# Expert down products in 32- and 64-token tiles, with another order of the last scatter and the last layer norm, in a one-core encoder layer

## Chip, cores and metric

One core of a Trainium2 chip (trn2) runs the whole program. The metric is the device time of one execution in microseconds (us); it stood at a median of 1172.59 us over 3 runs (1171.43 to 1172.86) before the change. All data are float32.

## What is computed

An encoder layer over two sequences that share all weights: a prompt of 256 tokens and a sample of 512 tokens, width 1024. In front stand a layer norm, an input projection, attention heads beside a two-way state-space scan, an output projection and a layer norm. The part that the change touches is the last one, the mixture of experts and the norm behind it:

```python
def _expert_choice(h, w_router, w_gate, w_up, w_down):
    n_tok, d = h.shape
    cap = CAPACITY_FACTOR * n_tok // N_EXPERTS
    aff = jax.nn.softmax((h @ w_router).astype(jnp.float32), axis=-1)
    gate, idx = lax.top_k(aff.T, cap)
    xe = h[idx]
    hid = jax.nn.silu(jnp.einsum("ecd,edf->ecf", xe, w_gate)) * jnp.einsum("ecd,edf->ecf", xe, w_up)
    ye = jnp.einsum("ecf,efd->ecd", hid, w_down) * gate[..., None].astype(h.dtype)
    return jnp.zeros_like(h).at[idx.reshape(-1)].add(ye.reshape(-1, d))
...
    moe = _expert_choice(x.reshape(b * s, d), w_router, w_e_gate, w_e_up, w_e_down).reshape(b, s, d)
    ple = jax.nn.sigmoid(x @ w_ple_gate + b_ple_gate) * (p @ w_ple)
    return _layer_norm(DN_ALPHA * x + moe + ple, ln2_g, ln2_b)
```

There are 16 experts of 1024 x 1024 weights for gate, up and down. Each expert takes its 32 best prompt tokens and its 64 best sample tokens, 96 rows together.

## The kernel before

The tokens are six tiles of 128: two of the prompt (TP = 2), four of the sample. `x1_rows` and `acc_rows` are arrays in HBM. `acc_rows` holds, for every token, everything that the last norm will read: it starts as the scaled residual plus the gated embedding, and the experts' rows are added to it.

For each expert the engines pass a piece of work on, ordered by semaphores alone, in hand-written loops (one `Fori` on each engine):

- **SP** issues the weight loads: four quarters of gate and up weights (`load_gu`, 2 MB each, into four buffers `gu_w`), two halves of the down weights (`load_dn`, 2 MB each, into two buffers `dn_w`). A load waits until TensorE has finished with what is in its buffer (`s_ug` for a quarter, `s_ud` for a half).
- **POOL** gathers the 96 rows from `x1_rows` (`gather`) and later scatters the expert's output rows with an add (`scatter`, L683).
- **PE** (TensorE) turns the gathered rows (`rows_turn`, L1911), multiplies by gate and up (`gate_up`, L1933), turns the hidden rows (`hid_turn`, L1919) and multiplies by down (`down_half`, L1945).
- **ACT** applies silu (L996) and copies turned rows (L728); **DVE** multiplies silu and up (`hidden`, L1419), copies the turned hidden rows (`hid_out`, L1413) and multiplies the down products by the gates (`ye_out`, L1426).

The 96 rows are three groups of 32. A product has 128 contraction rows, 32 stationary columns (the tokens) and a slice of the weights as moving operand; four such products, one for each quarter of the weight columns, write PSUM partitions 0, 32, 64 and 96 and run side by side in four column tiles of the array. In `down_half`:

```python
for i in range(4):
    k = 4 * d + i
    for g in range(NG3):
        for j in range(CT):
            last = nc.tensor.matmul(ps[32 * j:32 * (j + 1), DN + g, 0:256], src[:, k, 32 * g:32 * (g + 1)],
                                    dn_w[d][:, i, 256 * j:256 * (j + 1)], start=(k == 0), stop=(k == KD - 1))
```

That is 8 x 3 x 4 = 96 products an expert. Partition 32 j + t of a group holds quarter j of token t's output row, so a scatter of one group writes 128 pieces of 256 elements; there are three scatters an expert. The turns (L1911, L1919) use the array whole (128 columns).

The down weights of expert 15 go into the same two buffers `dn_w`, each when `down` of expert 14 has finished with it. `hid_turn` of expert 15 stands between the halves of `down` of expert 14. When all scatters have landed, SP loads the six tiles of `acc_rows` into `fin`, and the last norm runs through them: DVE statistics (`stats_half`, `moments`, `variance`), a square root on ACT (L1011), DVE `inverse` and `shift`, one pass on ACT (L1013), two halves of the gain on DVE (L1467), the bias on POOL (L715, the last tile on DVE, L1498), and the store (L558).

Of the kernel before, what the change touches and what calls it, by code (L numbers as in the profile page):

```python
# [20 lines left out]
ALU = mybir.AluOpType  # L21
# [7 lines left out]
P = 128  # L29
# [36 lines left out]
def hymba_layer(nc, A, consts, out_prompt, out_sample):  # L66
# [8 lines left out]
    NG3 = CAP // 32  # L75
    PADW = TP * P + TS * P + 6
# [6 lines left out]
    with ctx:  # L83
        def sb(name, shape, dt=F32):
            return ctx.enter_context(nc.sbuf_tensor(name, shape, dt))
# [41 lines left out]
        jcol = sb("jcol", [P, 1])  # L127
        idx4 = sb("idx4", [P, NG3, NE], I32)
        idxT = sb("idxT", [CAP, NE], I32)
        idx_now = sb("idx_now", [P, 1 + NG3], I32)  # L130
# [64 lines left out]
        gate4 = att[:, 0, 0:NG3 * NE].rearrange("p (i e) -> p i e", i=NG3)  # L195
# [7 lines left out]
        dn_w = [slot[j].rearrange("p (k c) -> p k c", k=4) for j in (5, 2)]  # L203

# [137 lines left out]
        s_bn = sem("s_bn")  # L342
        s_mv = sem("s_mv")
        s_inv = sem("s_inv")
        s_ln_s = sem("s_ln_s")
        s_ln_z = sem("s_ln_z")
        s_ln_g = sem("s_ln_g")
        s_y2 = sem("s_y2")
        s_y2_last = sem("s_y2_last")
# [85 lines left out]
        def _(sp):  # L435
# [108 lines left out]
            for d in range(2):  # L544
                sp.wait_ge(s_ud, 2 * (NE - 2) + d + 1)
                load_dn(NE - 1, d)

            sp.wait_ge(s_scat, 16 * NG3 * NE)
            for t in range(NT):
                sp.dma_start(fin[:, t, :], acc_rows[t * P:(t + 1) * P, :]).then_inc(s_fin[t], 16)  # L550
            for t in range(NT):
                if t + 1 < NT:
                    sp.wait_ge(s_y2, t + 1)
                else:
                    sp.wait_ge(s_y2_last, 1)
# [10 lines left out]
        def _(pool):  # L566
            ch = Chain(pool, s_pool)
            ch.link(nc.gpsimd.memset(ones[:], 1.0))
            for j in range(CT):
                ch.link(nc.gpsimd.memset(jcol[32 * j:32 * (j + 1), :], float(j)))  # L570
# [110 lines left out]
            def scatter():  # L681
                for i in range(NG3):
                    pool.indirect_dma_start(acc_quarters,  # L683
                                            bass.IndirectOffsetOnAxis(ap=idx_now[:, 1 + i:2 + i], axis=0),
                                            ye[:, i, :], None, compute_op=ALU.add).then_inc(s_scat, 16)
# [4 lines left out]
            def pick_quarters(e):  # L690
                return nc.gpsimd.tensor_copy(idx_now[:, 1:1 + NG3].unsqueeze(2), idx4[:, :, bass.ds(e, 1)])  # L691
# [16 lines left out]
            for e in (NE - 3, NE - 2, NE - 1):  # L708
# [10 lines left out]
        def _(act):  # L719
# [289 lines left out]
            for t in range(NT):  # L1009
                root()  # L1010
                nc.scalar.activation(sd[:, 0, t:t + 1], sd[:, 0, t:t + 1], ACT.Sqrt).then_inc(s_std, 1)  # L1011
                act.wait_ge(s_ln_s, t + 1)
                nc.scalar.activation(fin[:, t, :], fin[:, t, :], ACT.Identity, bias=mv[:, t, 1:2],  # L1013
                                     scale=sd[:, 1, t:t + 1]).then_inc(s_ln_z, 1)
# [3 lines left out]
        def _(dve):  # L1018
# [366 lines left out]
            for (a, n), c0, cap in ((SEQS[0], 0, CAPP), (SEQS[1], CAPP, CAPS)):  # L1385
                lo, hi = a * P, (a + n) * P
                for k in range(cap // 8):
# [6 lines left out]
                    if rounds % 4 == 0:  # L1394
# [8 lines left out]
            nc.vector.tensor_scalar(idx4[:].rearrange("p i e -> p (i e)"), ps[:, 5, NE:(1 + NG3) * NE], float(CT), jcol[:, 0:1],  # L1403
                                    ALU.mult, ALU.add).then_inc(s_idx, 1)
            nc.vector.tensor_copy(att[:, 0, 0:NG3 * NE], ps[:, 5, (1 + NG3) * NE:(1 + 2 * NG3) * NE]).then_inc(s_idx, 1)
# [15 lines left out]
            def ye_out(e, at_e, first=False):  # L1421
                dve.wait_ge(s_ud, 2 * (e + 1))
                if not first:
                    dve.wait_ge(s_scat, 16 * NG3 * e)
                for i in range(NG3):
                    last = nc.vector.tensor_scalar(ye[:, i, :], ps[:, DN + i, 0:256], gate4[:, i, at_e], None,  # L1426
                                                   ALU.mult)
                last.then_inc(s_ye, 1)
# [10 lines left out]
            ye_out(NE - 1, slice(NE - 1, NE))  # L1439

            def stats_half(t, half):
                dve.wait_ge(s_fin[t], 16)
                nc.vector.bn_stats(stats[:, t % 2, 6 * half:6 * half + 6],
                                   fin[:, t, half * 512:(half + 1) * 512]).then_inc(s_bn, 1)

            def moments(t):
                dve.wait_ge(s_bn, 2 * t + 2)
                nc.vector.bn_aggr(mv[:, t, :], stats[:, t % 2, :]).then_inc(s_mv, 1)

            def variance(t):  # L1450
                dve.wait_ge(s_mv, t + 1)
                nc.vector.tensor_scalar(sd[:, 0, t:t + 1], mv[:, t, 1:2], LN_EPS, None, ALU.add).then_inc(s_var, 1)

            def inverse(t):
                nroot[0] += 1
                dve.wait_ge(s_std, nroot[0])
                nc.vector.reciprocal(sd[:, 1, t:t + 1], sd[:, 0, t:t + 1]).then_inc(s_inv, 1)

            def shift(t):
                dve.wait_ge(s_inv, t + 1)  # L1460
                nc.vector.tensor_scalar(mv[:, t, 1:2], mv[:, t, 0:1], sd[:, 1, t:t + 1], -1.0, ALU.mult,
                                        ALU.mult).then_inc(s_ln_s, 1)

            def gain_half(t, half):
                dve.wait_ge(s_ln_z, t + 1)
                c = slice(half * 512, (half + 1) * 512)
                ins = nc.vector.tensor_tensor(fin[:, t, c], fin[:, t, c], gB[:, c], ALU.mult)  # L1467
                if half:
                    ins.then_inc(s_ln_g, 1)

            dve.wait_ge(s_ln2, 32)
            stats_half(0, 0)
            stats_half(0, 1)
            moments(0)
            variance(0)
            stats_half(1, 0)
            inverse(0)
            stats_half(1, 1)
            shift(0)
            moments(1)  # L1480
            variance(1)
            for t in range(NT):
                if t + 2 < NT:
                    stats_half(t + 2, 0)
                if t + 1 < NT:
                    inverse(t + 1)
                if t + 2 < NT:
                    stats_half(t + 2, 1)
                if t + 1 < NT:
                    shift(t + 1)  # L1490
                gain_half(t, 0)
                if t + 2 < NT:
                    moments(t + 2)
                gain_half(t, 1)
                if t + 2 < NT:
                    variance(t + 2)
            dve.wait_ge(s_ln_g, NT)
            nc.vector.tensor_tensor(fin[:, NT - 1, :], fin[:, NT - 1, :], bB[:], ALU.add).then_inc(s_y2_last, 1)  # L1498
# [3 lines left out]
        def _(pe):  # L1502
# [394 lines left out]
            for v, src in enumerate((topf, topv)):  # L1897
                for i in range(NG3):
                    c = (1 + v * NG3 + i) * NE
                    for j in range(CT):  # L1900
                        last = nc.tensor.matmul(ps[32 * j:32 * (j + 1), 5, c:c + NE], src[:, i * 32:(i + 1) * 32],
                                                ident[0:NE, 0:NE], start=True, stop=True)
# [35 lines left out]

            def down_half(e, d, src):
                pe.wait_ge(s_dnw[d], 16 * (e + 1))  # L1940
                for i in range(4):
                    k = 4 * d + i
                    for g in range(NG3):
                        for j in range(CT):
                            last = nc.tensor.matmul(ps[32 * j:32 * (j + 1), DN + g, 0:256],  # L1945
                                                    src[:, k, 32 * g:32 * (g + 1)],
                                                    dn_w[d][:, i, 256 * j:256 * (j + 1)],
                                                    start=(k == 0), stop=(k == KD - 1))
                last.then_inc(s_ud, 1)
# [34 lines left out]
            down(NE - 1, xeT)  # L1984
# [27 lines left out]
```

## Time and profile before

| what | us |
|---|---|
| median of 3 runs | 1172.59 (1171.43 to 1172.86) |
| the profiled execution's own time | 1173.55 |
| its span, first to last instruction | 1171.6 |
| PE busy (share of the span) | 1057.4 (90%) |
| DVE busy | 441.1 (38%) |
| POOL busy | 287.7 (25%) |
| ACT busy | 255.4 (22%) |
| start of expert 0's gate and up products | 591.25 |
| end of the last down product | 1128.32 |

The page is one execution. "Busy" is time with at least one instruction on the engine; PE is the matrix products, PEld the loads of their stationary operand, which overlap them. A product here is recorded twice, so 96 products are 192 records. "x1 (96*128)" shapes read as contraction rows * stationary columns, then the moving operand. The chain of waits is followed back from the last instruction; the timeline lists instructions by their start, neighbours of one line merged.

### The profile page before, as it was taken

How to read it: one execution, taken by the hardware profiler on the slowest of the kernel's cores; microseconds unless marked ns; L12 is line 12 of the kernel's file. 1: busy time of each engine (PE TensorE's matmuls, PEld its weight loads, DVE VectorE, ACT ScalarE, POOL GpSimd, SP SyncE). 2: the span in 40 equal slices, each digit the busy share in tenths (PEclk: the TensorE clock that was granted, in tenths of full speed). 3: DMA queues.
4: the chain of work that ended last, by engine and by line, in shares of the span. 5: the costliest groups of instructions: out<-in, count | busy, mean ns of one | idle time of the engine just before them, and what ended most of it. 6: DMA issues, size and time to landing. Idle time of an engine off the chain costs nothing.

```text
span 1171.6 us, 20620 instructions
## 1 busy us (share of the span) xinstructions
PE 1057.4 (90%) x8753; PEld 600.2 (51%) x8753; DVE 441.1 (38%) x872; ACT 255.4 (22%) x534; POOL 287.7 (25%) x311
## 2 busy tenths in 40 slices
PE   5999778878999899898999999999999999999940
PEld 3568667665565587665633334444443334444420
DVE  5436785447777876675100101111101101111018
ACT  1143334266556611320110000000000000000002
POOL 0006994234554200000100212221012212220134
PEclk9999998979999999999999999999999999999975
DMA  9010200200000531404189999999999999999854
GB/s 339 14 51 22 72 1 1 74 34 1 1 1 1 170 127 54 180 27 180 41 333 400 391 386 391 384 398 401 388 390 399 390 385 387 394 399 404 325 157 176
DMA packets 63116, 254.00 MB, mean 217 GB/s; under 512 B 7383, under 2 KB 15447, under 8 KB 46686
## 3 DMA queue, kind: packets, MB, share of 16 engines
q1 hardware_dynamic: 52542, 234.48, 51.3%
q0 software_dynamic: 10528, 18.88, 6.5%
q8 instruction: 31, 0.51, 0.2%
q14 instruction: 15, 0.12, 0.0%
HBM read 237.62 MB, written 15.73 MB: 216 GB/s over the span
## 4 chain that ended last, share of the span: by engine, by line
PE 67%; DVE 13%; DMA 9%; POOL 6%; issue 2%; ACT 2%; SPq 0%; DVEq 0%; POOLq 0%; ACTq 0%
PE ps L1933 24%; PE ps L1945 11%; DMA ring<-in_w_e_up 7%; PE ps L1574 4%; PE ps L1680 2%; PE ps L1695 2%; PE ps L1568 2%; PE ps L1828 1%; PE ps L1785 1%; PE ps L1787 1%; PE ps L1786 1%; PE ps L1813 1%; PE ps L1814 1%; PE ps L1815 1%; DVE xT L1467 1%
## 5 line engine op out<-in xcount | busy, mean ns | idle before, releaser
L1933 PE MATMUL ps<-ring,mix 128*32 128x512 f32 x1536 | 170.7, 592 | 2.1 <-DMA ring<-in_w_e_up 2.1
L1933 PE MATMUL ps<-late,mix 128*32 128x512 f32 x1536 | 171.1, 593 | 0.0
L1419 DVE TENSOR_TENSOR mix<-mix,ps 128x768 f32<-128x768 f32 x16 | 15.3, 954 | 323.0 <-ACT mix L996 323.0
L996 ACT ACTIVATE mix<-ps 128x768 f32<-128x768 f32 x16 | 13.0, 811 | 480.3 <-PE ps L1933 480.3
L1933 PEld LDWEIGHTS ps<-ring,mix 128*32 128x32 f32 x1536 | 49.6, 110 | 117.9 <-issue 111.9
L1933 PEld LDWEIGHTS ps<-late,mix 128*32 128x32 f32 x1536 | 48.1, 110 | 109.1 <-issue 106.8
L1945 PE MATMUL ps<-late,mix 128*32 128x256 f32 x1536 | 87.9, 385 | 2.8 <-DMA late<-in_w_e_down 2.8
L1945 PE MATMUL ps<-ring,mix 128*32 128x256 f32 x1536 | 85.9, 379 | 0.0
L1426 DVE TENSOR_SCALAR mix<-ps,att 128x256 f32<-128x256 f32 x48 | 20.3, 478 | 161.7 <-PE ps L1945 161.7
L683 POOL DMA_INDIRECT acc_rows<-mix,idx_now x48 | 75.0, 1562 | 20.5 <-POOL idx_now L691 10.7
L1945 PEld LDWEIGHTS ps<-late,mix 128*32 128x32 f32 x1536 | 49.9, 111 | 35.5 <-DVE mix L1413 3.2
L1945 PEld LDWEIGHTS ps<-ring,mix 128*32 128x32 f32 x1536 | 50.5, 110 | 32.3 <-issue 0.2
L688 POOL COPY idx_now<-idxT 96x1 int32 (+1 forms) x14 | 2.5, 182 | 221.1 <-PE ps L1911 221.1
L691 POOL COPY idx_now<-idx 128x3 int32 (+1 forms) x16 | 3.0, 186 | 194.5 <-DVE mix L1426 194.5
L1574 PE MATMUL ps<-ring,xT 128*128 128x512 f32 x96 | 45.2, 626 | 1.2 <-ACT xT L728 1.2
L1657 PE MATMUL ps<-xT 128*128 128x512 f32 (+1 forms) x96 | 45.0, 555 | 1.3 <-issue 1.3
L1548 PE MATMUL ps<-xl,wh 128*128 128x512 f32 (+1 forms) x128 | 44.0, 344 | 0.0
L1813 PE MATMUL ps<-ring_r,xT_r 128*128 128x512 f32 x96 | 40.4, 421 | 1.6 <-DVE cst L1359 1.6
L852 ACT ACTIVATE ring<-ps,att 128x512 f32<-128x512 f32 (+1 forms) x48 | 29.4, 612 | 48.9 <-DVE att L1190 48.8
L1099 DVE SCALAR_TENSOR_TENSOR late<-late,cw 128x770 f32<-128x770 f32 x32 | 39.2, 1227 | 0.9
L1671 PE MATMUL ps<-cst,ring 128*128 128x128 f32 x160 | 28.0, 291 | 11.3 <-DVE gb_in L1198 5.4
L1814 PE MATMUL ps<-late_r,xT_r 128*128 128x512 f32 x96 | 37.5, 391 | 0.0
(295 smaller groups left out, 1793.0 us busy)
## 6 DMA issues: line engine op xcount, KB each, us to landing
late<-in_w_e_gate SPq DMA_DIRECT2D x32, 1024.0 KB, 19.2
late<-in_w_e_up SPq DMA_DIRECT2D x32, 1024.0 KB, 21.3
ring<-in_w_e_gate SPq DMA_DIRECT2D x32, 1024.0 KB, 18.7
ring<-in_w_e_up SPq DMA_DIRECT2D x32, 1024.0 KB, 20.9
late<-in_w_e_down SPq DMA_DIRECT2D x16, 2048.0 KB, 22.3
ring<-in_w_e_down SPq DMA_DIRECT2D x16, 2048.0 KB, 22.2
ring<-in_w_in SPq DMA_DIRECT2D x3, 2048.0 KB, 9.0
late<-in_w_ple_gate SPq DMA_DIRECT2D x2, 2048.0 KB, 14.1
```

The lines of the kernel that those rows point to most:

```text
L683: pool.indirect_dma_start(acc_quarters, bass.IndirectOffsetOnAxis(ap=idx_now[:, 1 + i:2 + i], axis=0), ye[:, i, :], None, compute_op=ALU.a ...
L852: nc.scalar.activation(prob[:, u % 4, 0:L], ps[:, u % 3, 0:L], ACT.Exp, bias=att[:, 0, u:u + 1], scale=HD ** -0.5, accum_out=att[:, 1, u:u ...
L1099: ins = nc.vector.scalar_tensor_tensor(conv[:, m, :], u_pad[:, m, j:j + CW], cw[:, m, j:j + 1], conv[:, m, :], ALU.mult, ALU.add)
L1548: nc.tensor.matmul(o, w_h, xl[:, k, a * P:(a + w) * P], start=False, stop=False)
L1568: last = nc.tensor.matmul(bank[:, 0:272], lhs[k], wkv[:, k, :], start=(k == 0), stop=(k == KD - 1))
L1574: last = nc.tensor.matmul(bank, lhs[k], slotk[0][:, k, :], start=(k == 0), stop=(k == KD - 1))
L1657: nc.tensor.matmul(ps[:, u % 3, 0:n * P], qT[:, h % 4, t * P:(t + 1) * P], kz[:, h // 4, a * P:(a + n) * P], start=True, stop=True).then_i ...
L1671: last = nc.tensor.transpose(ps[:, 3, b * P:(b + 1) * P], prob[:, u % 4, b * P:(b + 1) * P], ident)
L1813: nc.tensor.matmul(o, x_h, wpg_h[h][:, k, :], start=(k == 0), stop=False)
L1814: nc.tensor.matmul(o, x_h, wpg_l[h][:, k, :], start=False, stop=False)
L1933: last = nc.tensor.matmul(ps[32 * j:32 * (j + 1), GU + g, :].rearrange("p (w c) -> p w c", w=2), xeT[:, k, 32 * g:32 * (g + 1)], gu_w[q][: ...
L1945: last = nc.tensor.matmul(ps[32 * j:32 * (j + 1), DN + g, 0:256], src[:, k, 32 * g:32 * (g + 1)], dn_w[d][:, i, 256 * j:256 * (j + 1)], st ...
```

## The change

Four edits. The down products of an expert are made in two groups instead of three: the 32 prompt tokens as before, in four tiles of 32 columns with 256 moving columns, and the 64 sample tokens in two tiles of 64 columns with 512 moving columns. There are two scatters an expert: 128 pieces of 256 elements and 128 pieces of 512. The down weights of expert 15 are loaded into two of the gate and up buffers, once expert 15's own first two quarters are used. Expert 15 makes all prompt products first; its prompt rows are scaled, scattered, loaded and normed ahead of its sample rows. The last norm is two `scalar_tensor_tensor` passes over a tile on DVE; its statistics come from DVE for the first tile of each sequence and from ACT, by two accumulating passes, for the other four; POOL does none of it.

```diff
@@ names @@
-        hid, ye = [r.rearrange("p (i c) -> p i c", i=NG3) for r in rows[2:4]]
-        acc_quarters = acc_rows.rearrange("t (j c) -> (t j) c", j=CT)
+        hid = rows[2].rearrange("p (i c) -> p i c", i=NG3)
+        ye = (rows[3][:, 0:256], rows[3][:, 256:768])
+        acc_parts = (acc_rows.rearrange("t (j c) -> (t j) c", j=4), acc_rows.rearrange("t (j c) -> (t j) c", j=2))
...
+        dn_last = [slot[j].rearrange("p (k c) -> p k c", k=4) for j in (3, 0)]
@@ SP @@
             for d in range(2):
-                sp.wait_ge(s_ud, 2 * (NE - 2) + d + 1)
-                load_dn(NE - 1, d)
-
-            sp.wait_ge(s_scat, 16 * NG3 * NE)
+                sp.wait_ge(s_ug, 4 * (NE - 1) + d + 1)
+                sp.dma_start(dn_last[d], wd[NE - 1, :, 4 * d:4 * d + 4, :]).then_inc(s_dn_last[d], 16)
+
+            for i, tiles in enumerate((range(TP), range(TP, NT))):
+                sp.wait_ge(s_scat, 16 * NSC * (NE - 1))
+                sp.wait_ge(s_scat_last[i], 16)
+                for t in tiles:
+                    sp.dma_start(fin[:, t, :], acc_rows[t * P:(t + 1) * P, :]).then_inc(s_fin[t], 16)
@@ POOL @@
-            pool.wait_ge(s_scat, 16 * NG3 * NE)
-            for t in range(NT - 1):
-                pool.wait_ge(s_ln_g, t + 1)
-                nc.gpsimd.tensor_tensor(fin[:, t, :], fin[:, t, :], bB[:], ALU.add).then_inc(s_y2, 1)
+            pool.wait_ge(s_scat, 16 * NSC * (NE - 1))
+            ch.link(pick_quarters(NE - 1))
+            for i in range(NSC):
+                pool.wait_ge(s_ye, NE + i)
+                pool.indirect_dma_start(acc_parts[i], bass.IndirectOffsetOnAxis(ap=idx_now[:, 1 + i:2 + i], axis=0),
+                                        ye[i], None, compute_op=ALU.add).then_inc(s_scat_last[i], 16)
@@ ACT @@
+            def row_mean(t):
+                act.wait_ge(s_fin[t], 16)
+                ch.link(nc.scalar.activation(junk, fin[:, t, :], ACT.Copy, accum_out=mv[:, t, 0:1]))
+                ch.link(nc.scalar.activation(mv[:, t, 1:2], mv[:, t, 0:1], ACT.Copy, scale=-1.0 / D))
+
+            def row_std(t):
+                ch.link(nc.scalar.activation(junk, fin[:, t, :], ACT.Square, bias=mv[:, t, 1:2],
+                                             accum_out=sd[:, 0, t:t + 1]))
+                nc.scalar.activation(sd[:, 0, t:t + 1], sd[:, 0, t:t + 1], ACT.Sqrt, bias=epsc[:],
+                                     scale=1.0 / D).then_inc(s_std, 1)
+
+            x_std(0)
+            row_mean(1)
+            row_std(1)
+            row_mean(TP + 1)
+            x_std(TP)
+            row_std(TP + 1)
+            for t in range(TP + 2, NT):
+                row_mean(t)
+                row_std(t)
@@ DVE @@
-            ye_out(NE - 1, slice(NE - 1, NE))
...
+            dve.wait_ge(s_scat, 16 * NSC * (NE - 1))
+            for i, w in enumerate((256, 512)):
+                dve.wait_ge(s_ud, 2 * NE - 1 + i)
+                nc.vector.tensor_scalar(ye[i], ps[:, DN + i, 0:w], gate4[:, i, NE - 1:NE], None,
+                                        ALU.mult).then_inc(s_ye, 1)
+
+            def last_norm(t):
+                nroot[0] += 1
                 dve.wait_ge(s_std, nroot[0])
...
+                ch.link(nc.vector.reciprocal(sd[:, 1, t:t + 1], sd[:, 0, t:t + 1]))
+                mean, op = (mv[:, t, 0:1], ALU.subtract) if t in (0, TP) else (mv[:, t, 1:2], ALU.add)
+                ch.link(nc.vector.scalar_tensor_tensor(fin[:, t, :], fin[:, t, :], mean, gB[:], op, ALU.mult))
+                nc.vector.scalar_tensor_tensor(fin[:, t, :], fin[:, t, :], sd[:, 1, t:t + 1], bB[:], ALU.mult,
+                                               ALU.add).then_inc(s_y2, 1)
...
             for t in range(NT):
...
+                if t in (0, TP):
+                    dve.wait_ge(s_fin[t], 16)
+                    ln_stats(t, fin[:, t, :], LN_EPS)
+                last_norm(t)
@@ PE @@
+            def down_step(g, k, src, w):
+                rows = (32, 64)[g]
+                cols = D * rows // P
+                for j in range(P // rows):
+                    last = nc.tensor.matmul(ps[rows * j:rows * (j + 1), DN + g, 0:cols], src[:, k, ROWS[g]],
+                                            w[:, cols * j:cols * (j + 1)], start=(k == 0), stop=(k == KD - 1))
+                return last
+
             def down_half(e, d, src):
                 pe.wait_ge(s_dnw[d], 16 * (e + 1))
                 for i in range(4):
...
+                    down_step(0, 4 * d + i, src, dn_w[d][:, i, :])
+                    last = down_step(1, 4 * d + i, src, dn_w[d][:, i, :])
                 last.then_inc(s_ud, 1)
...
-            down(NE - 1, xeT)
+            pe.wait_ge(s_hT, NE)
+            pe.wait_ge(s_ye, NE - 1)
+            for g in range(NSC):
+                for k in range(KD):
+                    if k % 4 == 0:
+                        pe.wait_ge(s_dn_last[k // 4], 16)
+                    last = down_step(g, k, xeT, dn_last[k // 4][:, k % 4, :])
+                last.then_inc(s_ud, 1)
```

How the instructions stand now, at the three places of which the prediction speaks. First PE in the loop over experts, from the turn of the next expert's rows to the end of `down`; `ps` is PSUM, `late` and `ring` hold the two down buffers, a shape is stationary columns x moving columns (a turn shows its moving operand's), x how many in a row. Before, and then the first rows of the change:

```order
L1911 MATMUL ps<-cst,mix 128x96 x8
L1954 REGISTER_ALU
L1940 REGISTER_ALU
L1945 MATMUL ps<-late,mix 32x256 x48
L1945 MATMUL ps<-ring,mix 32x256 x48
```

```order
L1896 MATMUL ps<-cst,mix 128x96 x8
L1942 REGISTER_ALU
L1933 REGISTER_ALU
L1928 MATMUL ps<-late,mix 32x256 x4
L1928 MATMUL ps<-late,mix 64x512 x2
```

The last two rows stand four times over `late` and four times over `ring`: eight groups of four products with eight groups of two between them, where 96 products of one kind stood in a row.

Second, the end of PE's program, expert 15 (the change alone; before it read as the loop does):

```order
L1928 MATMUL ps<-late,mix 32x256 x16
L1928 MATMUL ps<-ring,mix 32x256 x16
L1928 MATMUL ps<-late,mix 64x512 x8
L1928 MATMUL ps<-ring,mix 64x512 x8
L86 UNCONDITIONAL_BRANCH
```

Here all prompt products stand ahead of all sample products, and `late` and `ring` are gate and up buffers.

Third, DVE from the last gate multiplication on, in the change, with what each waits for (`xT` is the memory of `fin`, `s_ud` PE's down products, `s_scat` the landed scatters, `s_fin` a landed tile, `s_std` a square root on ACT, `s_dve` DVE's own result):

```order
L1465 TENSOR_SCALAR mix<-ps,att 128x256 [waits s_ud,s_scat]
L1465 TENSOR_SCALAR mix<-ps,att 128x512 [waits s_ud]
L1046 BN_STATS stats<-xT 128x6 [waits s_fin_0,s_ln2]
L1046 BN_STATS stats<-xT 128x6
L1049 BN_AGGR mv<-stats 128x2 [waits s_dve]
L1050 TENSOR_SCALAR sd<-mv 128x1 [waits s_dve]
L1471 RECIPROCAL sd<-sd 128x1 [waits s_std]
L1473 SCALAR_TENSOR_TENSOR xT<-xT,mv,gB 128x1024 [waits s_dve]
L1474 SCALAR_TENSOR_TENSOR xT<-xT,sd,bB 128x1024 [waits s_dve]
```

The statistics and the norm of tile 0 stand behind both gate multiplications of expert 15; the statistics of tile 2, the first of the sample, stand behind the norm of tile 1.

## Rows read from the trace of the kernel before

**Rows 1.** Page, the span in 40 slices: busy tenths of PE and of DMA.

```profile
PE   5999778878999899898999999999999999999940
...
DMA  9010200200000531404189999999999999999854
```

**Rows 2.** Chain of waits, one expert's round: start us, us, what.

```profile
913.01 20.74 PE ps L1933 x192
933.75 1.06 PE ps L1911 x8
934.81 10.50 PE ps L1945 x192
945.31 0.81 PE ps L1919 x6
```

**Rows 3.** Who waited for whom from 600 us on: total us, times, longest.

```profile
PE ps L1945 <- DMA late<-in_w_e_down: 2.8, 1, 2.8
...
PE ps L1933 <- DMA ring<-in_w_e_up: 2.1, 3, 1.0
```

**Rows 4.** Timeline of PE where tiles change: start us, us, line, shape, count.

```profile
933.14 0.61 PE L1933 MATMUL ps<-ring,mix 128*32 128x512 f32 x4
933.68 0.46 PE L1911 MATMUL ps<-cst,mix 96*128 96x96 f32 x2
...
934.54 0.27 PE L1911 MATMUL ps<-cst,mix 96*128 96x96 f32 x1
934.74 0.42 PE L1945 MATMUL ps<-late,mix 128*32 128x256 f32 x4
...
934.98 0.40 PE L1945 MATMUL ps<-late,mix 128*32 128x256 f32 x4
```

**Rows 5.** Timeline of PE, whole-array products around one-row products.

```profile
509.11 0.39 PE L1814 MATMUL ps<-late_r,xT_r 128*128 128x512 f32 x1
509.34 0.39 PE L1815 MATMUL ps<-ring_r,mix_r 128*128 128x512 f32 x1
509.65 0.50 PE L1823 MATMUL ps<-bB_r,ones_r 1*128 1x512 f32 x1
509.99 0.39 PE L1824 MATMUL ps<-gB_r,ones_r 1*128 1x512 f32 x1
```

**Rows 6.** Timeline of PE, 16 contraction rows, 96 and then 32 columns.

```profile
541.13 0.22 PE L1896 MATMUL ps<-cst 16*96 16x16 f32 x1 [2.03 <-DVE cst L1398]
541.28 0.38 PE L1901 MATMUL ps<-cst 16*32 16x16 f32 x24
```

**Rows 7.** Timeline of the end: the last experts' products, scatters, loads and norm.

```profile
1107.92 5.39 PE L1945 MATMUL ps<-ring,mix 128*32 128x256 f32 x96
...
1114.77 1.01 DVE L1413 COPY mix<-ps 128x384 f32<-128x384 f32 x2
...
1117.26 1.55 POOL L683 DMA_INDIRECT acc_rows<-mix,idx_now  x1 [0.30 <-issue]
...
1137.79 2.73 SPq L550 DMA_DIRECT2D xT<-acc_rows  x6
1141.11 1.28 DVE L1443 BATCH_NORM_STATS2 stats<-xT 128x6 f32<-128x512 f32 x2 [11.46 <-DMA xT<-acc_rows]
...
1143.34 0.15 DVE L1457 RECIPROCAL sd<-sd 128x1 f32<-128x1 f32 x1
...
1165.87 1.23 DVE L1498 TENSOR_TENSOR xT<-xT,bB 128x1024 f32<-128x1024 f32 x1
```

**Rows 8.** Chain of waits: the last scatter, from its issue to its landing.

```profile
1133.92 3.85 DMA acc_rows<-mix,idx_now
```

**Rows 9.** Groups by line and shape: count, then busy us, mean ns.

```profile
L1325 DVE SCALAR_TENSOR_TENSOR xa<-xa,ps 128x1024 f32<-128x1024 f32 x6 | 7.3, 1216 | 3.0 <-PE ps L1787 3.0
...
L1013 ACT ACTIVATE xT<-xT,mv,sd 128x1024 f32<-128x1024 f32 x6 | 7.4, 1240 | 6.3 <-DVE mv L1461 6.3
...
L852 ACT ACTIVATION_READ_ACCUMULATOR ring<-ps,att 128x1 f32 x48 | 9.2, 193 | 0.0
```

More of the change, by code:

```diff
@@ L75, in hymba_layer @@
     NG3 = CAP // 32
+    NSC = 2
+    ROWS = (slice(0, CAPP), slice(CAPP, CAP))
+    assert (CAPP, CAPS) == (32, 64)
     PADW = TP * P + TS * P + 6
@@ L341, in hymba_layer @@
         s_lgT = sem("s_lgT")
[L342 to L347, printed above, removed]
         s_y2 = sem("s_y2")
-        s_y2_last = sem("s_y2_last")
+        s_scat_last = [sem(f"s_scat_last{i}") for i in range(NSC)]
+        s_dn_last = [sem(f"s_dn_last{d}") for d in range(2)]
         s_out = sem("s_out")
@@ L544, in _ @@
             for d in range(2):
-                sp.wait_ge(s_ud, 2 * (NE - 2) + d + 1)
-                load_dn(NE - 1, d)
-            sp.wait_ge(s_scat, 16 * NG3 * NE)
-            for t in range(NT):
[L550 to L555, printed above, removed]
+                sp.wait_ge(s_ug, 4 * (NE - 1) + d + 1)
[5 more added lines that the diff above has]
+                    sp.dma_start(fin[:, t, :], acc_rows[t * P:(t + 1) * P, :]).then_inc(s_fin[t], 16)
+            for t in range(NT):
+                sp.wait_ge(s_y2, t + 1)
                 dst = out_prompt[0] if t < TP else out_sample[0]
@@ L681, in scatter @@
             def scatter():
-                for i in range(NG3):
-                    pool.indirect_dma_start(acc_quarters,
+                for i in range(NSC):
+                    pool.indirect_dma_start(acc_parts[i],
                                             bass.IndirectOffsetOnAxis(ap=idx_now[:, 1 + i:2 + i], axis=0),
-                                            ye[:, i, :], None, compute_op=ALU.add).then_inc(s_scat, 16)
+                                            ye[i], None, compute_op=ALU.add).then_inc(s_scat, 16)
             def pick_rows(e):
@@ L707, in _ @@
                 scatter()
-            for e in (NE - 3, NE - 2, NE - 1):
+            for e in (NE - 3, NE - 2):
                 pool.wait_ge(s_ye, e + 1)
@@ L1007, in _ @@
             silu(NE - 1)
[L1009 to L1014, printed above, removed]
+            junk = mixf[:, 0:D]
+            def row_mean(t):
[16 more added lines that the diff above has]
+                row_std(t)
         @block.vector
@@ L1423, in ye_out @@
                 if not first:
[L1424 to L1427, printed above, removed]
+                    dve.wait_ge(s_scat, 16 * NSC * e)
+                for i, w in enumerate((256, 512)):
+                    last = nc.vector.tensor_scalar(ye[i], ps[:, DN + i, 0:w], gate4[:, i, at_e], None, ALU.mult)
                 last.then_inc(s_ye, 1)
@@ L1438, in _ @@
             hid_out(NE - 1, xeT)
-            ye_out(NE - 1, slice(NE - 1, NE))
[L1441 to L1452, printed above, removed]
@@ L1454, in inverse @@
-            def inverse(t):
+            dve.wait_ge(s_scat, 16 * NSC * (NE - 1))
+            for i, w in enumerate((256, 512)):
+                dve.wait_ge(s_ud, 2 * NE - 1 + i)
+                nc.vector.tensor_scalar(ye[i], ps[:, DN + i, 0:w], gate4[:, i, NE - 1:NE], None,
+                                        ALU.mult).then_inc(s_ye, 1)
+            def last_norm(t):
                 nroot[0] += 1
                 dve.wait_ge(s_std, nroot[0])
-                nc.vector.reciprocal(sd[:, 1, t:t + 1], sd[:, 0, t:t + 1]).then_inc(s_inv, 1)
@@ L1459, in shift @@
[L1459 to L1469, printed above, removed]
@@ L1897, in _ @@
             for v, src in enumerate((topf, topv)):
[L1898 to L1901, printed above, removed]
+                for i in range(NSC):
+                    c = (1 + v * NSC + i) * NE
+                    w = ROWS[i].stop - ROWS[i].start
+                    for j in range(P // w):
+                        last = nc.tensor.matmul(ps[w * j:w * (j + 1), 5, c:c + NE], src[:, ROWS[i]],
                                                 ident[0:NE, 0:NE], start=True, stop=True)
```

59 lines of the change are left out of this document (17 added, 42 removed).

## Prediction

> **What bounds the kernel now.** I read the slices of the page first: from about half of the span PE and the DMA engines are both at 9 in nearly every slice, and only the last two or three slices empty out [rows 1]. That splits the change in two: a stage in which PE and DMA are both near their limit, and a tail.
>
> In the stage, the chain of waits says which of them ends last: a round of one expert is 20.74 us of gate and up products, 1.06 of turns, 10.50 of down products and 0.81 of turns, 33.1 us together, all on PE with no gap between [rows 2]. The weights come almost as fast: PE waited for gate and up weights three times, 2.1 us in all [rows 3]. So PE sets the pace, DMA is a hair behind, and whatever is added to PE's round is paid in full, by every expert.
>
> In the tail the timeline shows a string of steps that each wait for the one before. I count from T0, the end of expert 14's down products, 1107.92 + 5.39 = 1113.31 [rows 7]. The span ends at 1171.6, so the tail is 58.3 us.
>
> **The price of a down product.** 192 records are 48 sets of four neighbours: 10.50 / 48 = 0.219 us a set with 256 moving columns [rows 2]. Gate and up products have 512: 20.74 / 48 = 0.432 us a set [rows 2]. The change makes 16 sets of four with 256 columns (3.50 us) and 16 sets of two with 512 columns (6.91 us) an expert: 10.4 against 10.5 us. If two tiles of 64 columns run side by side as four of 32 do, streaming costs what it did; I put down nothing for it.
>
> **What changes of tile cost.** The new order goes from four tiles to two and back in every step of k. Where does PE change the way it divides the array today? Between gate and up products (32 columns) and turns (whole array): the last set starts at 933.14, the first turn at 933.68, 0.54 us later, though a set takes 0.43: 0.11 lost [rows 4]. Back again: 934.54 to 934.74, 0.20 us, where a turn takes about 0.12 (1.06 over 8, less the start); 0.08 lost, and the first set after it takes 0.24 instead of 0.22, 0.02 more [rows 4]. Within the products with 128 contraction rows a pair starts 0.23 us apart; into the one-row products it is 0.31 (0.08 lost), and the first of these takes 0.34 (0.11 lost) [rows 5]. The second loss is the load of the stationary columns, which cannot run ahead over the change: 0.02 us for 32 columns, 0.11 for 128. That column width alone does it shows in 541.13 to 541.28: 0.15 us behind a product of only 16 moving columns, while the 24 records that follow begin and end within 0.38 us [rows 6].
>
> None of these is a change from four tiles to two. The Trainium skill, "TensorEngine Tiling (Array Packing)", Tiling Modes, Key Properties, says that changing the mode, not just the tile, drains the engine; the rows agree with it for the whole array against tiles. By that rule four to two drains too and the sum below stands; where the rule does not reach so far, the time is the first rival's.
>
> For one change from 32 to 64 columns I take 0.10 for the change and 0.05 for the load of 64 columns (between the 0.02 of 32 and the 0.11 of 128): 0.15 us. Back to 32 columns: 0.10 + 0.02 = 0.12 us. An expert has eight of the first and seven of the second: 8 x 0.15 + 7 x 0.12 = 2.04 us. Experts 0 to 13 pay that, 28.6 us; expert 14 one change fewer, since a turn stands between its halves, 1.9; expert 15 one change, 0.15. Sum 30.6 us for 225 changes, 0.136 each. Bounds: 0.08, the smallest loss with its load hidden, makes 18 us; 0.08 + 0.11, rounded to 0.20, makes 45. I take the middle because the width lies in the middle. Nothing in these rows excludes zero for four to two, which is the first rival.
>
> **What goes.** With a round of 35.1 us the weights have 2 us more an expert, so the 2.1 us of waits go [rows 3]. Two scatters instead of three spare POOL an issue in each round; POOL waits for PE there, so nothing. Gate multiplications and copies on DVE and ACT lie beside PE's products.
>
> **The tail.** It loses steps one after another.
> - *Down weights of 15.* PE waited 2.8 us for them [rows 3]. But the turned hidden rows come only at 1114.77 + 1.01 = 1115.78 [rows 7], T0 + 2.5, so all but 0.3 us of that wait stays, with another thing late.
> - *Prompt products* end at 2.5 + 3.5 = T0 + 6.0. They are not what the prompt waits for: DVE also waits until expert 14's scatters have landed. The second issue, now the last, starts at 1117.26 [rows 7], T0 + 3.9; from the last issue to its landing it takes 3.85 us [rows 8]: T0 + 7.8.
> - *Prompt scatter.* Multiplication and issue some 0.75, landing 3.85: T0 + 12.4. From the load's issue at 1137.79 to the first statistics at 1141.11 it is 3.3 us [rows 7]: T0 + 15.7.
> - *Tile 0.* From statistics to the reciprocal 1143.34 - 1141.11 = 2.2; then 0.15 and two passes at 1.22 [rows 9], 2.6 us: done at T0 + 20.5.
> - *Tile 1.* ACT starts when tile 0's root is done, T0 + 17.7, and needs two passes of 1.24 with a read-out of 0.19 each [rows 9], and two small steps of 0.2: 3.3 us, T0 + 21.0. DVE 2.6: T0 + 23.6.
> - *Tile 2*, the first sample tile. Sample products end at 6.0 + 6.9 + 0.1 = T0 + 13.0, multiplication and issue 1.0, landing 3.85, load 3.3: T0 + 21.2. DVE reaches it at 23.6, so 2.4 us of slack hide a slower last product. Statistics and root 2.2: 25.8; passes: T0 + 28.4.
> - *Tiles 3 to 5.* ACT needs 3.3 us a tile and has tile 3 ready before 28.4, tiles 4 and 5 just before DVE, which needs 2.6, comes to them: tile 3 at 31.0, tile 4 at 33.6, tile 5 at 36.4.
> - *The end.* Last pass to end of span was 1171.6 - (1165.87 + 1.23) = 4.5 [rows 7]: T0 + 40.9.
>
> 58.3 - 40.9 = 17.4 us saved, give or take 3.
>
> **Sum.** 30.6 - 2.1 - 17.4 = 11.1 us longer. The profiled execution took 1173.55 us, 0.96 above the median of the runs, so 1184.7 on its own terms and, for the median, 1172.6 + 11.1 = 1183.7: I say 1184. With the bounds of the change of tile, 18 and 45 us, the sum runs from -1.5 to +25.5: the forecast's own range is 1171 to 1198.
>
> **The rivals.**
> - *Four tiles to two is free.* The break-even is 19.5 / 225 = 0.087 us a change; below it the tail decides and the kernel is faster. At nothing, the stage keeps its pace of 33.1 us, DMA stays a hair behind, and the 2.1 us of waits may stay or go. Expert 15's weights then come no earlier than DMA can bring them, about 1.5 us after PE wants the second half. Saved: 16 to 19.5 us, 1153 to 1157, say 1155. For it: all tiles of both kinds have 128 contraction rows, and within 32 columns no set waits. Against it: in rows 4 to 6 each change of width cost something.
> - *A small price*, 0.03 to 0.08 us a change: 7 to 18 us against 19.5, 1160 to 1171.
> - *Two tiles of 64 do not run side by side.* The sample's 6.9 us become 13.8 in each of 16 experts: 110 us, near 1290. No row shows tiles of 64 columns; four of 32 run side by side in every one, so I hold this for unlikely.
> - *The prompt's lead does not come about* (its rows wait for something else than expert 14's scatter). Then the norm alone gets shorter, the tail saves some 10 us, and the forecast becomes 1191, inside its own range.
>
> **How the numbers follow.** Forecast with its bounds 0.70; free change 0.20; small price 0.06; no side by side 0.04. A measurement of this kernel can tell 0.2%, 2.3 us, from no change. Faster by more: the free change, and most of the small price: 0.25. Within: the prices around break-even: 0.05. Slower: the rest of the forecast and the last case: 0.70. The forecast alone leaves out 3 in 10, with the small price still more than 2 in 10, so the range reaches down to the free change: 1153 to 1198. The likeliest case's own range is 1171 to 1198.
>
> **What the new profile would show.** A round of 35.1 us in the chain of waits, with down products of about 12.5 us instead of 10.50; in the timeline of PE, starts of a four-tile set and the next two-tile set further apart than 0.22 and 0.43 us, by 0.15 and 0.12. No wait of PE for gate and up weights. In the tail, two loads of prompt tiles ahead of the last scatter's landing, and some 41 us from the last down product of expert 14 to the end. The forecast is wrong if the down products of a round stay at 10.5 us: then the changes were free. It is wrong by size if the round is right and the tail is not near 41.

## The result and the profile after

The changed kernel takes 1187.17 us (median of 4 runs, 1185.25 to 1187.70) where the kernel before took 1172.58: a ratio of 1.0123, 95% interval 1.0106 to 1.0141. Slower by 14.6 us; 1184 was forecast. The profiled execution took 1185.25 us with a span of 1183.4, 11.8 us longer than before; 11.1 was the sum. It was the fastest of the four runs and the account below goes by it, so some 2.8 us of the 14.6 lie outside that account.

The chain of waits of the changed kernel, one expert's round (start us, us, what), answers to [rows 2]:

```profile
932.55 20.74 PE ps L1918 x192
953.29 1.06 PE ps L1896 x8
954.35 12.63 PE ps L1928 x96
966.98 0.81 PE ps L1904 x6
```

Three of the four pieces are what they were to a hundredth. The down products grew from 10.50 to 12.63 us although there are half as many of them. The round is 35.2 us, all on PE.

The timeline of PE at the start of one expert's down products, one row for each set of products that start together (start us, us, line, shape, count of records):

```profile
919.05 0.42 PE L1928 MATMUL ps<-late,mix 128*32 128x256 f32 x4
919.29 0.40 PE L1928 MATMUL ps<-late,mix 128*32 128x256 f32 x4
919.62 0.65 PE L1928 MATMUL ps<-late,mix 128*64 128x512 f32 x2
920.10 0.60 PE L1928 MATMUL ps<-late,mix 128*64 128x512 f32 x2
920.63 0.42 PE L1928 MATMUL ps<-late,mix 128*32 128x256 f32 x4
920.87 0.40 PE L1928 MATMUL ps<-late,mix 128*32 128x256 f32 x4
```

Read the distances of the starts against 0.22 us for a set of 256 columns and 0.43 for one of 512. From four tiles to two: 0.33 instead of 0.22, and the first set of two then takes 0.48 instead of 0.43: 0.11 + 0.05 = 0.16 us. Back: 0.53 instead of 0.43, and 0.24 instead of 0.22: 0.10 + 0.02 = 0.12 us. A step of k is 1.58 us where the sets alone need 1.30.

Who waited for whom from 600 us on (total us, times, longest), against [rows 3]:

```profile
DVE mix L1465 <- DMA acc_rows<-mix,idx_now: 6.3, 1, 6.3
...
PE ps L1928 <- DVE mix L1437: 2.4, 1, 2.4
...
PE ps L1918 <- DMA late<-in_w_e_up: 0.4, 1, 0.4
```

PE's three waits for gate and up weights, 2.1 us, are gone. The 0.4 us is a new wait, among expert 1's gate and up products, ahead of the first longer round: those rounds give DMA time. Its wait in front of expert 15's down products is still 2.4 us, no longer for the weights but for DVE's copy of the turned hidden rows.

The timeline of the end, against [rows 7]; T0, the end of expert 14's products, is 1136.42 + 6.34 = 1142.76 by the chain, which is shown behind it:

```profile
1145.10 3.44 PE L1928 MATMUL ps<-late,mix 128*32 128x256 f32 x32 [2.37 <-DVE mix L1437]
...
1146.51 1.55 POOL L685 DMA_INDIRECT acc_rows<-mix,idx_now  x1 [0.30 <-issue]
...
1150.38 3.65 PE L1928 MATMUL ps<-late,mix 128*64 128x512 f32 x16
...
1151.31 0.48 DVE L1465 TENSOR_SCALAR mix<-ps,att 128x256 f32<-128x256 f32 x1 [6.26 <-DMA acc_rows<-mix,idx_now]
...
1152.54 1.55 POOL L718 DMA_INDIRECT acc_rows<-mix,idx_now  x1 [1.01 <-DVE mix L1465]
...
1153.87 3.60 PE L1928 MATMUL ps<-ring,mix 128*64 128x512 f32 x16
...
1157.52 0.75 DVE L1465 TENSOR_SCALAR mix<-ps,att 128x512 f32<-128x512 f32 x1 [5.72 <-PE ps L1928]
...
1159.68 1.29 DVE L1046 BATCH_NORM_STATS2 stats<-xT 128x6 f32<-128x512 f32 x2 [1.42 <-DMA xT<-acc_rows]
...
1166.06 1.28 DVE L1474 SCALAR_TENSOR_TENSOR xT<-xT,sd,bB 128x1024 f32<-128x1024 f32 x1
1167.27 1.28 DVE L1046 BATCH_NORM_STATS2 stats<-xT 128x6 f32<-128x512 f32 x2
1167.81 1.06 ACT L1019 ACTIVATE mix<-xT 128x1024 f32<-128x1024 f32 x1 [3.29 <-DMA xT<-acc_rows]
...
1179.11 1.28 DVE L1474 SCALAR_TENSOR_TENSOR xT<-xT,sd,bB 128x1024 f32<-128x1024 f32 x1
```

```profile
1136.42 6.34 PE ps L1928 x48
...
1145.10 12.39 PE ps L1928 x96
...
1158.55 4.73 DMA acc_rows<-mix,idx_now
...
1169.22 0.21 ACT sd L738
```

From 1142.76 to the end of the span it is 40.6 us, where it was 58.3. So the change cost 29.5 us ahead of T0 (1142.76 - 1113.31) and saved 17.7 behind it.

### The profile page after: what moved, and what is told of

Its sections match the earlier page's. It is cut to its first block, busy times and chain, and to the rows that moved or that the text cites. A ratio compares the mean times of both kernels' runs of the same rounds, so it can differ in the third digit from the quotient of the medians.

```text
span 1183.4 us, 17451 instructions
## 1 busy us (share of the span) xinstructions
PE 1089.4 (92%) x7193; PEld 549.6 (46%) x7193; DVE 433.7 (37%) x834; ACT 258.2 (22%) x548; POOL 250.9 (21%) x295
## 4 chain that ended last, share of the span: by engine, by line
PE 75%; DVE 12%; POOL 5%; DMA 3%; ACT 2%; issue 2%; SPq 0%; DVEq 0%; POOLq 0%; ACTq 0%
PE ps L1918 27%; PE ps L1928 17%; PE ps L1558 4%; PE ps L1664 2%; PE ps L1679 2%; PE ps L1552 2%; DMA late<-in_w_e_up 2%; PE ps L1812 1%; PE ps L1896 1%; PE ps L1769 1%; PE ps L1770 1%; PE ps L1771 1%; PE ps L1797 1%; PE ps L1798 1%; PE ps L1799 1%
## 5 line engine op out<-in xcount | busy, mean ns | idle before, releaser
L1928 PE MATMUL ps<-late,mix 128*32 128x256 f32 (+1 forms) x768 | 102.8, 475 | 2.4 <-DVE mix L1437 2.4
L1918 PEld LDWEIGHTS ps<-ring,mix 128*32 128x32 f32 x1536 | 49.9, 110 | 114.9 <-issue 114.3
L1928 PE MATMUL ps<-ring,mix 128*32 128x256 f32 (+1 forms) x768 | 101.5, 467 | 0.0
L1918 PEld LDWEIGHTS ps<-late,mix 128*32 128x32 f32 x1536 | 48.2, 110 | 109.3 <-issue 108.0
L1450 DVE TENSOR_SCALAR mix<-ps,att 128x256 f32<-128x256 f32 (+1 forms) x30 | 17.1, 613 | 180.4 <-PE ps L1928 180.4
L1928 PEld LDWEIGHTS ps<-ring,mix 128*32 128x32 f32 (+1 forms) x768 | 23.7, 118 | 76.1 <-issue 75.7
L1928 PEld LDWEIGHTS ps<-late,mix 128*32 128x32 f32 (+1 forms) x768 | 23.9, 119 | 69.7 <-issue 65.0
L685 POOL DMA_INDIRECT acc_rows<-mix,idx_now x30 | 46.8, 1561 | 15.0 <-POOL idx_now L693 10.5
L693 POOL COPY idx_now<-idx 128x2 int32 (+1 forms) x16 | 3.0, 185 | 221.5 <-DVE mix L1450 218.2
L1799 PE MATMUL ps<-ring_r,mix_r 128*128 128x512 f32 x96 | 38.0, 396 | 0.0
## 6 DMA issues: line engine op xcount, KB each, us to landing
late<-in_w_ple_gate SPq DMA_DIRECT2D x2, 2048.0 KB, 14.7
```

What stands on the lines that cost most here:

```text
L685: pool.indirect_dma_start(acc_parts[i], bass.IndirectOffsetOnAxis(ap=idx_now[:, 1 + i:2 + i], axis=0), ye[i], None, compute_op=ALU.add).th ...
L1799: nc.tensor.matmul(o, x_l, wpg_h[h][:, k, :], start=False, stop=False)
L1918: last = nc.tensor.matmul(ps[32 * j:32 * (j + 1), GU + g, :].rearrange("p (w c) -> p w c", w=2), xeT[:, k, 32 * g:32 * (g + 1)], gu_w[q][: ...
L1928: last = nc.tensor.matmul(ps[rows * j:rows * (j + 1), DN + g, 0:cols], src[:, k, ROWS[g]], w[:, cols * j:cols * (j + 1)], start=(k == 0), ...
```

## The experiments

The theory to test: each change between 32- and 64-column tiles costs PE some 0.14 us (2.13 us over 15 changes), and the rest of the change is a gain. The rival for the loss: products with 64 columns are slow in themselves. In one series the kernel before ran beside the first four kernels (median 1173.81 us), in a second beside the last two (1173.70).

**Two steps of k together.** Same products, other order:

```diff
                 for i in range(4):
-                    down_step(0, 4 * d + i, src, dn_w[d][:, i, :])
-                    last = down_step(1, 4 * d + i, src, dn_w[d][:, i, :])
+                for i0 in range(0, 4, 2):
+                    for g in range(NSC):
+                        for i in range(i0, i0 + 2):
+                            last = down_step(g, 4 * d + i, src, dn_w[d][:, i, :])
```

> The changed kernel, but in a half of the down products two steps of k of the 32-column products stand together, then two of the 64-column products: 7 changes of tile an expert in place of 15. Theory (each change of tile costs 0.14 us of PE time, as 12.63 - 10.50 = 2.13 us over 15 changes in the changed kernel's chain): down products of a round 10.50 + 7 x 0.142 = 11.5 us, 8 x 0.142 x 15 = 17 us less in all, 1170 us, up to 1172 if waits for weights come back. Rival (the 64-column products are slow in themselves, whatever stands beside them): down products stay at 12.6, 1187 us.

Measured: 1169.99 us, 0.9963 (0.9947 to 0.9978) of the kernel before. The chain of waits of this kernel has for one expert's down products:

```profile
912.59 11.47 PE ps L1928 x96
```

11.47 us where 11.5 was expected. Nothing but the order of the same products changed, so the rival falls.

**Four steps of k together**, a half of the weights at a time: the same edit with 4 in place of 2.

> The changed kernel, but in each half of the down products all four steps of k of the 32-column products stand first and then all four of the 64-column products: 3 changes of tile an expert. Theory: down products of a round 10.50 + 3 x 0.142 = 10.9 us, 12 x 0.142 x 15 = 25.6 us less, 1161.6 us, up to 1164 if PE waits for weights again. Rival (64-column products slow in themselves): 12.6 and 1187 us.

Measured: 1161.33 us, 0.9887 (0.9871 to 0.9904). The same row of its chain:

```profile
907.22 10.90 PE ps L1928 x96
```

With 3, 7 and 15 changes the down products take 10.90, 11.47 and 12.63 us: 0.14 us for each change from the first step to the second (0.57 over 4) and 0.145 from the second to the third (1.16 over 8). A straight line.

Two other things change together with the tile, and rows of the kernel before show both to be free. One is the PSUM bank (`DN + g`): there it changes behind every set of four products, and a set of 256 columns still takes 0.22 us [rows 2]. The other is the number of moving columns. In the products of the input projection it goes from 256 to 512 while the array stays whole (timeline of PE):

```profile
106.17 0.28 PE L1549 MATMUL ps<-xh_b,wl 128*128 128x256 f32 x1
106.28 0.40 PE L1547 MATMUL ps<-xh_a,wh 128*128 128x512 f32 x1
106.51 0.39 PE L1548 MATMUL ps<-xl,wh 128*128 128x512 f32 x1
```

The first product of 512 columns starts 0.11 us after the last of 256, where products of 256 stand 0.12 apart, and the next one 0.23 later, the usual distance.

**Three groups of 32.** The change without its tiles of 64 columns: three groups of products, three scatters, everything else of the change kept.

```diff
-                rows = (32, 64)[g]
-                cols = D * rows // P
-                for j in range(P // rows):
-                    last = nc.tensor.matmul(ps[rows * j:rows * (j + 1), DN + g, 0:cols], src[:, k, ROWS[g]],
-                                            w[:, cols * j:cols * (j + 1)], start=(k == 0), stop=(k == KD - 1))
+                for i in ((0,), (1, 2))[g]:
+                    for j in range(CT):
+                        last = nc.tensor.matmul(ps[32 * j:32 * (j + 1), DN + i, 0:256], src[:, k, 32 * i:32 * (i + 1)],
+                                                w[:, 256 * j:256 * (j + 1)], start=(k == 0), stop=(k == KD - 1))
```

> The changed kernel with the sample's 64 tokens as two groups of 32 columns in four tiles, and so three scatters an expert, as before the change; the early weights of expert 15, its prompt rows first and the two-pass norm stay. No change of tile inside the down products. Theory: down products 10.50 us and a tail of about 41 us instead of 58.3: 1172.6 - 17.7 = 1155 us, 1153 to 1157 by what the waits for weights do. Rival (the shorter tail hangs on the two scatters and the 64-column products, with three scatters the sample's rows land 2 to 4 us later and DVE waits for them): 1157 to 1160 us.

Measured: 1157.93 us, 0.9861 (0.9845 to 0.9878): faster than both kernels, by 15.9 us than the kernel before in the same series. That lies a little above the theory's 1153 to 1157 and in the rival's range, but not for the rival's reason. The chain of waits and the waits of PE of this kernel:

```profile
903.32 10.50 PE ps L1926 x192
...
1120.74 3.76 DMA acc_rows<-mix,idx_now
1124.53 0.49 DVE mix L1464
...
1141.01 1.21 DVE stats L1045 x2
```

```profile
PE ps L1926 <- DVE mix L1436: 2.5, 1, 2.5
PE ps L1917 <- DMA ring<-in_w_e_up: 2.2, 3, 0.8
```

The down products are back at 10.50 us and the waits for weights at 2.2. DVE's statistics of the first sample tile start at 1141.01 straight behind tile 1, so the sample's rows were not late. What is late is the prompt: it waits for the third scatter of expert 14, issued at 1120.74, which has no counterpart in the changed kernel. From the end of expert 14's products, 1114.98, to the end of the span (1157.0) it is 42.0 us, 1.4 more than with two scatters. With that the saving of 17.7 becomes 16.3; 15.9 were measured. The agreement is no closer than 1 us: in the profiled execution expert 0's products already start 1.3 us later than before (592.56 against 591.25), ahead of every product that was changed.

**The products alone.** The kernel before with 32- and 64-column products in turn and two scatters, also for expert 15; its weights, order and norm as before. The edit to the products is that of the change:

```diff
-                    for g in range(NG3):
-                        for j in range(CT):
...
+                    down_step(0, 4 * d + i, src, dn_w[d][:, i, :])
+                    last = down_step(1, 4 * d + i, src, dn_w[d][:, i, :])
```

> The kernel before with only the products and scatters of the change: 32- and 64-column products in turn, two scatters an expert, also for expert 15; its weights, its order and the last norm as before. Theory: 14 x 15 + 14 + 15 = 239 changes at 0.142 us are 34 us, less 2.1 us of waits for weights and some 2 us for one scatter less at the end: 1172.6 + 30 = 1202 us. Rival (part of the 14.6 us that the whole change cost comes from the edits to the tail): 1190 us or less.

Measured: 1203.97 us, 1.0251 (1.0234 to 1.0268), 30.2 us more than the kernel before beside it where the theory has 30; the rival falls. The two halves of the change add up: 1.0251 x 0.9861 = 1.011, against 1.0123 (1.0106 to 1.0141) for the whole.

**An earlier prompt.** The kernel with three groups points to where the rest of its tail lies: the prompt's scatter waits for the sample's rows of expert 14, though prompt and sample share no row. The core of the edit, on DVE, POOL and PE:

```diff
+            hid_out(NE - 2, hidT)
+            hidden(NE - 1)
             hid_out(NE - 1, xeT)
+            ye_out(NE - 2, slice(NE - 2, NE - 1))
...
+            put(idx_now[:, 1:1 + NSC], ye[0], 0, s_scat14[0])
+            put(idx_now[:, 1:1 + NSC], ye[1], 1, s_scat14[1])
+            pool.wait_ge(s_scat14[0], 16)
+            pool.wait_ge(s_ye, NE)
+            put(idx_last, ye_last[0], 0, s_scat_last[0])
+            put(idx_now[:, 1:1 + NSC], ye[2], 2, s_scat14[1])
...
-                    last = down_step(g, k, xeT, dn_last[k // 4][:, k % 4, :])
+                    last = down_step(g, k, xeT, dn_last[k // 4][:, k % 4, :], DN=GU)
```

> The kernel with three groups of 32 (e3_three) with a shorter way to the first prompt tile: DVE copies expert 15's turned hidden rows before it scales expert 14's products; expert 15's down products go to the PSUM banks of gate and up and its scaled rows to the memory of the hidden rows, so that PE need not wait behind expert 14; the prompt scatter of expert 15 waits for the prompt scatter of expert 14 alone (prompt and sample rows are never the same). Theory (in the tail the prompt's path sets the end, and it is held by the landing of expert 14's last scatter, 1124.5 in e3_three): that landing moves to about 1121.1, the multiplication is done by then, so the prompt's scatter lands at 1125.0 instead of 1129.6: 4.6 us less, some 0.5 given back because ACT's third tile lands later: 1154 us. Rival (DVE's and ACT's passes or the sample's rows already set the end, the lead does not matter): 1157 to 1158 us.

Measured: 1156.79 us, 0.9860 (0.9843 to 0.9876); beside the kernel with three groups, 0.9861, no difference that can be told. The theory's 1154 is missed; the time is the rival's, whose reading holds in part. The waits of PE, the timeline and the chain of waits of this kernel show why:

```profile
PE ps L1932 <- DMA ring<-in_w_e_up: 2.4, 3, 1.0
PE ps L1941 <- DMA ring<-in_w_e_down: 2.1, 1, 2.1
```

```profile
1114.96 1.91 PE L1941 MATMUL ps<-late,mix 128*32 128x256 f32 x32
...
1118.94 3.62 PE L1941 MATMUL ps<-ring,mix 128*32 128x256 f32 x32 [2.07 <-DMA ring<-in_w_e_down]
...
1122.63 0.48 DVE L1479 TENSOR_SCALAR mix<-ps,att 128x256 f32<-128x256 f32 x1 [6.15 <-PE ps L1941]
...
1127.82 10.25 SPq L555 DMA_DIRECT2D xT<-acc_rows  x6
...
1132.61 1.28 DVE L1058 BATCH_NORM_STATS2 stats<-xT 128x6 f32<-128x512 f32 x2 [2.20 <-DMA xT<-acc_rows]
```

```profile
1118.94 10.57 PE ps L1941 x160
...
1132.62 3.70 DMA acc_rows<-mix,idx_last
...
1140.95 1.16 ACT mix L1031 x2
```

PE now runs straight from expert 14 into expert 15, catches up with the last 2 MB of weights, waits 2.1 us for them, and does the next set of products at half its pace (3.62 us for 32 records that took 1.91; the granted clock from 1120.0 to 1122.3 was 0.50). The multiplication that was to be done by 1121.1 starts at 1122.63, 1.9 us earlier than with three groups. Behind it the way from the load of the first tile to the first statistics takes 4.8 us (1127.82 to 1132.61) where it took 3.6 (1129.60 to 1133.24). The first statistics start at 1132.61 instead of 1133.24: 0.6 us gained of 4.6.

The end then hangs on the sample, as the rival had it. Its products wait behind the same weights, its last scatter is issued at 1132.62 instead of 1130.73, and the chain that ended last runs from that scatter through ACT's pass over tile 3. The wait that was removed became a wait for DMA.

**No head start.** Three groups of 32, but no tile is loaded before the last scatter has landed:

```diff
-                sp.wait_ge(s_scat_last[i], 16 * (i + 1))
+                sp.wait_ge(s_scat_last[0], 16)
+                sp.wait_ge(s_scat_last[1], 32)
```

> The kernel with three groups of 32 (e3_three), but SP loads no tile of the last norm before the last scatter has landed. Theory (the head start of the prompt rows is worth the distance from the prompt's landing at 1129.6 to the sample's at about 1134.5): 4.9 us more, 1162.8 us; so of the 17.7 us that the tail saves 5 are the head start and 13 the norm and the early weights. Rival (the norm's DVE passes overlap the sample's landing so well only by chance, ACT then delays tile 2): no more than 1159 us, or more than 1165.

Measured: 1163.58 us, 0.9921 (0.9902 to 0.9940), 5.7 us more than with the head start (each a median of four runs, of two series). The theory had 4.9 and 1162.8 us; the time lies between the rival's two bounds, so the rival falls. By the two traces the tail is 46.5 us against 42.0, 4.5 more. So of the tail's gain some 4.5 to 6 us are the prompt's head start.

The other 11.8 us (58.3 - 46.5) can be divided by the chain of waits, against [rows 8]:

```profile
1109.67 5.36 PE ps L1927 x96
...
1117.52 10.61 PE ps L1927 x192
...
1130.76 3.80 DMA acc_rows<-mix,idx_now
```

T0 is here 1115.03. From the landing of the last scatter to the end of the span it is 26.9 us (1134.56 to 1161.5), where it was 33.8 (1137.77 to 1171.6): 6.9 us are the norm's. The landing itself lies 19.5 us behind T0 instead of 24.5: expert 15's products end 2.0 us earlier, and its prompt rows are scattered by then. The early weights were not tried apart.

## Why the prediction was right

**The bound.** PE set the pace and DMA stood right behind it. Both halves showed: PE's longer products were paid in full in every round (35.2 us, 35.1 forecast), and where they are short again PE's waits for weights return, 2.2 us with three groups and 2.4 in the kernel with the earlier prompt.

**The price of a change of tile.** Forecast 0.15 and 0.12 us, taken from changes between the whole array and tiles of 32 [rows 4 to 6]; measured 0.16 and 0.12. Even the parts came out: 0.11 and 0.10 for the change (0.10 forecast), 0.05 for the load of 64 columns, 0.02 for 32. The 0.05 was a guess between 0.02 and 0.11, and that it came out is partly luck. Ahead of T0 the sum was 30.5 - 2.1 = 28.4 us; measured 29.5. The products grew by 31.8 us, as 15 experts pay some 0.09 us more than the 2.04 put down; the waits gave back the other 2.4. The Trainium skill, "TensorEngine Tiling (Array Packing)", Tiling Modes, Key Properties, says that a change of the tiling mode drains the engine; the rows agree with it for four tiles against two, 0.11 and 0.10 us lost at each change. The first rival, a free change, is excluded by the orders with 3, 7 and 15 changes, and the price is inside the forecast's bounds.

**Streaming put down as nothing.** Two tiles of 64 do run side by side: within expert 15, where no change comes between, eight sets start from 1150.38 to 1153.87, 0.44 us each, where four tiles of 32 took 0.43 for 512 columns. That rival is gone too.

**The tail.** Forecast 40.9 us, measured 40.6, but as a sum of errors that cancel, which is luck. The steps in us behind T0:

| step | forecast | measured |
|---|---|---|
| PE starts expert 15's products | 2.5 | 2.3 |
| expert 14's scatters landed (DVE goes on) | 7.8 | 8.6 |
| sample products end | 13.0 | 14.7 |
| first statistics | 15.7 | 16.9 |
| tile 1 done | 23.6 | 24.6 |
| tile 5 done | 36.4 | 37.6 |
| end of span | 40.9 | 40.6 |

The landing is the first mis-sized term: 3.85 us was taken from a scatter of 256-element pieces [rows 8], while the second scatter has pieces of 512, which took 4.8 from its issue at 1146.51 to DVE's start. The second is the multiplication and the issue of the prompt's scatter, 1.23 us from 1151.31 to 1152.54 where 0.75 was put down. Everything behind keeps some 1.1 us. The end gives it back: from the last pass to the end of the span it was 4.5 us before and is 3.0 now; why the last store is quicker was not tried.

That the slack of 2.4 us for the sample's rows hides a slower last product did not quite hold. The products took 12.4 us instead of 10.5, so tile 3 reached ACT only at 1167.81, 0.5 us after DVE had begun with tile 2's statistics at 1167.27. ACT's first steps on tile 3 stand ahead of tile 2's root in its program, and the root began at 1169.22, though its input was ready at 1168.97. The chain that ended last therefore runs through the sample's products, scatter and load, and no longer through the prompt's: the slack was overrun by some 0.2 us.

**The prompt's lead** came about as forecast; taken away it costs 5.7 us by the medians and 4.5 by the traces, where its rival had it at 17.4 - 10 = 7.4.

## What to carry to other kernels

Where products of different tile widths share the array, put all of one width together: every change between widths costs about 0.14 us here, and 15 of them an expert turned a gain of 16 us into a loss of 15. Or keep to one width: here the wider tiles gained nothing themselves, and three groups of 32 (1157.93 us) beat even 3 changes an expert (1161.33). Price such a change from the changes that the trace already holds (into a transpose, out of it), by the distance of starts against the pace inside a run. And before shortening a wait at the end, look at what else arrives just then: with PE and DMA this close, PE ran into the weights instead, and the sample's rows, not far behind the prompt's, set the end.

## What the runs showed that was not expected

The weights' time from issue to landing fell by more than half once PE's round was 2 us longer. The DMA part of the page of the changed kernel (KB each, us to landing):

```profile
late<-in_w_e_up SPq DMA_DIRECT2D x32, 1024.0 KB, 8.7
ring<-in_w_e_up SPq DMA_DIRECT2D x32, 1024.0 KB, 10.3
```

The first of these rows before:

```profile
late<-in_w_e_up SPq DMA_DIRECT2D x32, 1024.0 KB, 21.3
```

The time goes with PE's round. For `late` it is 20.0 us with three groups (a round of 33.1 us), 18.0 with four steps together (33.5), 14.7 with two (34.1) and 8.7 here (35.2). At the 390 GB/s or so that the page before has in these slices 1 MB takes some 2.7 us, so most of the 21 us was probably spent behind other loads; that is an estimate, and no view shows the queue itself. PE's waits came to only 2.1 us at the same time: the landing time was the clearer sign of how near the second limit was.

A wait of 2.4 us in front of PE can cost PE a second time. The windows of the changed kernel behind that wait (us, busy time and count of PE, PEld, DVE, ACT, POOL, then the granted clock, DMA share, GB/s):

```profile
1145.10:1146.00 0.90, 0.90 (x12) 0.56 (x16) 0.00 (x0) 0.00 (x0) 0.90 (x1) 0.65 0.00 0
1146.00:1147.00 1.00, 1.00 (x12) 0.43 (x8) 0.00 (x0) 0.00 (x0) 0.69 (x2) 0.50 0.42 19
1147.00:1148.00 1.00, 1.00 (x16) 0.56 (x12) 0.00 (x0) 0.00 (x0) 1.00 (x1) 0.50 0.81 112
```

PE stood idle from 1142.76 to 1145.10, and the clock was then granted at 0.50, that is 1.2 GHz, until past 1148: the first 32 records took 3.44 us, the next 32 took 2.15.

It does not happen every time, and the kernel's time need not show it. With four steps of k together PE waited the same 2.37 us, the clock then stayed at 1.00 (2.4 GHz), and the same 32 records took 1.93 us:

```profile
1121.09 1.93 PE L1928 MATMUL ps<-late,mix 128*32 128x256 f32 x32 [2.37 <-DVE mix L1437]
```

Yet from the end of expert 14's products to the end of the span it is 40.7 us there and 40.6 here: what PE lost lay beside the prompt's path. After PE's wait at expert 15's products the clock fell in five of the profiled executions (the kernel before, the change, two steps together, the products alone, the earlier prompt), after waits of 2.1 to 2.8 us; it did not in the other three, whose waits were 2.4 to 2.5 us. So the length of the wait alone does not decide it, and what does was not tried.
